# Other places in SBUF, modulo 256 bytes, for the operands of a block matmul stream

## The reference

```python
xn = _rmsnorm(h, norm_w)
proj = jnp.einsum('bsd,de->bse', xn, w_in).astype(f32)      # 2048 -> 14352 columns
q, k, v_m, o_m, z_m, i_pre, f_pre, u_g, v_g, z_g = _split_cols(proj)
...                                                          # mLSTM of 8 heads, gated unit of 8 heads
y = jnp.concatenate([y_m, y_g], axis=-1).astype(x.dtype)
h = h + jnp.einsum('bse,ed->bsd', y, w_out)                  # 4096 -> 2048
```

## Time and profile before

| | |
|---|---|
| median of 3 runs | 3193.33 us (3190.05 to 3199.09) |
| profiled execution | 3189.83 us, its span 3188.3 us |
| PE busy | 3127.2 us, 98% of the span |
| granted clock of TensorE | 0.996 of full speed over the span |
| block stages: SGU, mLSTM, output | 185 to 555, 555 to 1263, 1313 to 1428.5 us |

### The profile page before, as it was taken

One profiled execution on the slowest core, in us unless ns is written; L12 is line 12 of the kernel. 1 busy time (PEld: TensorE's weight loads), 2 busy tenths in 40 slices (PEclk: granted clock), 3 DMA queues, 4 the chain that ended last, 5 costly groups with the idle time before them and its releaser, 6 DMA issues.

```text
span 3188.3 us, 59876 instructions
## 1 busy us (share of the span) xinstructions
PE 3127.2 (98%) x23182; PEld 2929.1 (92%) x23182; DVE 2205.0 (69%) x2929; ACT 1548.3 (49%) x2506; POOL 334.4 (10%) x343
## 2 busy tenths in 40 slices
PE   8999999999999999999989999999999999999998
PEld 6899999999999998898889999999998888888898
DVE  7678888888888888876775656656457456556535
ACT  5355555555555556442263655556226455545421
POOL 1000000000000000000000341350000124313000
PEclk9999999999999999999999999999999999999999
DMA  6234444434434345453334222223324322222432
GB/s 208 89 96 106 113 112 112 126 92 112 113 98 118 93 118 178 121 160 106 106 117 135 62 73 81 81 75 106 113 94 151 103 79 80 80 74 68 165 97 90
DMA packets 461728, 342.81 MB, mean 108 GB/s; under 512 B 20504, under 2 KB 451544, under 8 KB 458352
## 3 DMA queue, kind: packets, MB, share of 16 engines
q1 hardware_dynamic: 443712, 296.28, 32.3%
q0 software_dynamic: 8304, 26.92, 2.4%
q10 hardware_dynamic: 9552, 17.37, 1.6%
HBM read 315.04 MB, written 25.46 MB: 107 GB/s over the span
## 4 chain that ended last, share of the span: by engine, by line
PE 82%; DVE 6%; DMA 4%; DVEq 3%; issue 2%; ACT 2%; SPq 0%; ACTq 0%
PE ps L756 13%; PE ps L757 13%; PE ps L758 13%; PE ps L926 8%; PE ps L929 8%; PE ps L928 8%; DMA w_raw_blocks<-in_w_in 3%; PE ps L1179 2%; PE ps L1340 1%; PE ps L1342 1%; PE ps L1338 1%; PE ps L762 1%; PE ps L996 1%; PE ps L764 1%; PE ps L763 1%
## 5 line engine op out<-in xcount | busy, mean ns | idle before, releaser
L756 PE MATMUL ps<-x_high,w_high 128*128 128x264 f32 (+3 forms) x2880 | 913.7, 317 | 19.7 <-DVE x_low L2590 10.7
L757 PE MATMUL ps<-x_low,w_high 128*128 128x264 f32 (+3 forms) x2880 | 882.6, 306 | 0.0
L758 PE MATMUL ps<-x_high,w_low 128*128 128x264 f32 (+3 forms) x2880 | 880.9, 306 | 0.0
L2101 DVE TENSOR_TENSOR w_low<-w_raw,w_high 128x1024 fp32r<-128x1024 f32 x308 | 377.8, 1233 | 330.2 <-ACT w_high L1380 315.0
L756 PEld LDWEIGHTS ps<-x_high,w_high 128*128 128x128 f32 x2880 | 544.1, 189 | 52.1 <-issue 22.4
L757 PEld LDWEIGHTS ps<-x_low,w_high 128*128 128x128 f32 x2880 | 544.3, 189 | 28.0 <-issue 3.3
L758 PEld LDWEIGHTS ps<-x_high,w_low 128*128 128x128 f32 x2880 | 542.5, 188 | 24.8
L926 PE MATMUL ps<-x_high_rows,w_high_blocks 128*128 128x256 f32 x1792 | 507.5, 283 | 4.2 <-DVE u_gelu L2224 2.9
L928 PE MATMUL ps<-x_low_rows,w_high_blocks 128*128 128x256 f32 x1792 | 498.8, 278 | 0.0
L929 PE MATMUL ps<-x_high_rows,w_low_blocks 128*128 128x256 f32 x1792 | 498.8, 278 | 0.0
L1380 ACT ACTIVATE w_high<-w_raw 128x1024 fp32r<-128x1024 f32 x308 | 324.7, 1056 | 277.3 <-PE ps L758 202.4
(11 more groups left out here) (523 smaller groups left out, 5328.5 us busy)
## 6 DMA issues: line engine op xcount, KB each, us to landing
w_raw_blocks<-in_w_in SPq DMA_DIRECT2D x200, 512.0 KB, 5.0
w_raw<-in_w_in SPq DMA_DIRECT2D x384, 256.0 KB, 3.1
w_raw<-in_w_out SPq DMA_DIRECT2D x224, 256.0 KB, 3.0
w_raw_blocks<-in_w_out SPq DMA_DIRECT2D x24, 512.0 KB, 5.6
residual<-residual_stream ACTq DMA_DIRECT2D x8, 1056.0 KB, 10.4
residual_stream<-y_layer ACTq DMA_DIRECT2D x2, 2176.0 KB, 11.6
x_natural<-in_x SPq DMA_DIRECT2D x4, 1024.0 KB, 9.4
x_feature_major<-x_stage POOLq DMA_DIRECT2D x4, 1024.0 KB, 7.9
```

Source lines behind the costliest of these rows:

```text
L756: pe.matmul(dst, wh[:, j, kt, wc], x_hi[:, k, tok], start=first, stop=False)
L757: pe.matmul(dst, wh[:, j, kt, wc], x_lo[:, k, tok], start=False, stop=False)
L758: return pe.matmul(dst, wl[:, j, kt, wc], x_hi[:, k, tok], start=False, stop=last)
L2101: dve.tensor_tensor(wl[:, j], raw[:, j], f(wh[:, j]), ALU.subtract).then_inc(lo_ready, 1)
```

## The change

No instruction is added, taken away or moved: each engine has the same instructions in the same order (line numbers of the new kernel are 7 to 11 higher). What changes are addresses. The weight slots are put 4,112 bytes apart in place of 4,096, so that slot 0 to 3 start at 128, 144, 160 and 176 modulo 256, in `whb` and `wlb` alike. The activations stay at 64. S2 goes to 128, S1 to 192, S3 to 0; S3 of the output stage stays at 64. `w_low` moves on by 256 bytes and `w_raw` by 512, both still at 128. Everything behind them moves by a few hundred bytes: the scratch tensors of the first layer from 64 mostly to 0 or 32, the residual stream and `y_layer` of the later layers from 64 to 128, with the small tensors of attention at 32, 64, 96, 128, 160, 192 or 224. `x_high`, `x_low`, `w_high` and `w_low`, the operands of the plain units, keep their places modulo 256, but for the last piece of weights (`w_high_last`, 64 to 128).

Moving minus stationary becomes, for slot j: 192-16j with the activations, 0-16j (modulo 256) with S2, 64-16j with S1, 128-16j with S3. These are the 16 multiples of 16, one for each of the pairs; in the mLSTM stage every kind of block meets every slot. From a block to the next the difference changes, while before it never did.

```diff
+        r0.at += 256
         wl_at = r0.at
         wl = r0.take("w_low", [P, 4, 4, 256], F32R)
+        r0.at += 256
         raw_at = r0.at
...
-        whb = nc.alloc_sbuf_tensor_at("w_high_blocks", [P, 4, KH, P], F32R, offset=wh_at)
-        wlb = nc.alloc_sbuf_tensor_at("w_low_blocks", [P, 4, KH, P], F32R, offset=wl_at)
+        def slots_at(name, at_):
+
+            room = nc.alloc_sbuf_tensor_at(name, [P, 4 * KH * P + 16], F32R, offset=at_)
+            slot = lambda j: slice(j * (KH * P + 4), j * (KH * P + 4) + KH * P)
+            return [room[:, slot(j)].rearrange("p (k n) -> p k n", k=KH) for j in range(4)]
+
+        whb, wlb = slots_at("w_high_blocks", wh_at), slots_at("w_low_blocks", wl_at)
...
-        ROWS_AT = 64
-        big = r0.at + (ROWS_AT - r0.at) % 256
-        x1_at = [at_ + (ROWS_AT - at_) % 256 for at_ in (xh_at, xl_at)]
+        def placed(at_, residue):
+            return at_ + (residue - at_) % 256
+
+        R_X, R_S2, R_S1, R_S3, R_S3_OUT = 64, 128, 192, 0, 64
+        big = placed(r0.at, R_S2)
+        x1_at = [placed(at_, R_X) for at_ in (xh_at, xl_at)]
...
-        ym_at = big + KT * S * 4
+        ym_at = big + KT * S * 4 + 64
...
-        work = ym_at + KT * S * 4
+        work = ym_at + KT * S * 4 + 96
...
-        for n, name in ((B_S2, "s2"), (B_S1, "s1"), (B_S3, "s3")):
+        for n, name, residue in ((B_S2, "s2", R_S2), (B_S1, "s1", R_S1), (B_S3, "s3", R_S3)):
+            rx_.at = placed(rx_.at, residue)
...
-        rs = Region(big + 6 * BLOCK)
+        rs = Region(rx_.at)
...
-        work2 = r2.at
+        work2 = r2.at + 160
...
-        S3G = big + 77824
+        S3G = placed(rn.at + BLOCK, R_S3_OUT)
...
-                    w_hi, w_lo = whb[:, slots[i]], wlb[:, slots[i]]
+                    w_hi, w_lo = whb[slots[i]], wlb[slots[i]]
...
-                act.activation(whb[:, slot], weight(s, i), ACT.Copy).then_inc(hi_ready, 1)
+                act.activation(whb[slot], weight(s, i), ACT.Copy).then_inc(hi_ready, 1)
...
-                dve.tensor_tensor(wlb[:, slot], weight(s, i), f(whb[:, slot]), ALU.subtract).then_inc(lo_ready, 1)
+                dve.tensor_tensor(wlb[slot], weight(s, i), f(whb[slot]), ALU.subtract).then_inc(lo_ready, 1)
```

## The result

The changed kernel takes 3205.80 us (median of 7 executions, 3203.97 to 3208.87), the kernel before 3195.48 us on the same chip (7 executions, 3190.05 to 3199.09): a ratio of 1.0034 with a 95% interval of 1.0025 to 1.0044. That is 10.3 us slower, a little past the 0.3% within which the prediction counted a time as the same. The profiled execution of the changed kernel took 3207.86 us.

What follows compares the result with a forecast made beforehand. PE's matmul pace was taken to bound the kernel (busy 3127.2 of 3188.3 us). The block stream's +2.6 us, other parts 0, on the 3193.33 us median gave 3196, written as 3195 us; range 3171 to 3216 us.

Steps and rivals of the forecast that it cites:

- the case that was called likeliest: Whole kernel: same time within 0.3%, at 3195 us, from even fresh landings or places that don't matter; chance 0.37 together.
- every other relation is heavy: Block matmuls: only difference 192 has the quick pace, others run at 117.8 ns; +21 us, 3203 to 3214 us, chance 0.26.
- the all-quick to the all-heavy end: Block stream: all blocks at 113.3 ns (quick) saves 21 us; all at 117.8 ns (heavy) loses 21 us.
- the sum: Whole kernel: all priced parts together, +2.6 us from the block stream and 0 from the others.
- the block stream: The 9,408 block matmuls: half the blocks land heavy as now, the other half start with three heavy matmuls; +2.6 us.
- The landing itself: At each of 392 block boundaries the changed difference makes the stream take a pace afresh, without a wait, neither preferred.
- places don't matter: Block stream: paces depend on when PE starts after a wait and last until the next; 3193 us, chance 0.12.
- Which stages: Block stages before the change: heavy share 0.19 in SGU, 0.74 in mLSTM and 0.13 in the output stage.
- What is late next: mLSTM: DVE's 2.7 us per block nearly level with all-quick PE's 2.72; a few of 18 us come back as waits.
- the rivals on the fast side: Block stream: shifts at boundaries end heavy runs but not quick ones; 3172 to 3183 us, chance 0.34.
- the writes to the slots: DVE's and ACT's writes at 16-byte steps: 0 us, low part stays 1,219 ns; slowed writes cost 10 us or more, chance 0.03.
- the other tensors: Attention's and the output's small tensors moved by multiples of 32: under 1 us, taken as 0.

Runs made afterwards that it cites:

- experiment 7: Changed kernel with all weight slots at 0, activations and sums at 64, so difference 64 in every block: 3202.72 us, ratio 1.0036 to the kernel before.
- experiment 1: Changed kernel with all slots at 144, activations and sums at 64, so difference 176 in every block: 3208.95 us against 3192.51 for the kernel before.
- experiment 2: Changed kernel with all slots back at 128, only the sums moved (differences 192, 0, 64, 128): 3202.45 us, ratio 1.0031 to the kernel before.
- experiment 5: Changed kernel with only the slots moved, all moving rows at 64 (differences 192, 176, 160, 144): 3204.27 us, ratio 1.0043 to the kernel before.
- experiment 6: Changed kernel with only slot 3 moved, 48 bytes on (difference 144, others 192), moving rows at 64: 3195.34 us, ratio 1.0010 to the kernel before.
- experiment 11: Changed kernel with slots at 140, 148, 152, 156, moving rows at 64 (differences 180, 172, 168, 164): 3200.71 us, ratio 1.0029 to the kernel before.
- experiment 9: Changed kernel with all slots at 140, activations and sums at 64, so difference 180 in every block: 3190.54 us against 3192.19 for the kernel before.
- experiment 3: Changed kernel with all slots at 160, activations and sums at 96, so difference 192 kept in every block: 3191.85 us, ratio 0.9995 to the kernel before.

## Why the prediction was right and where it was wrong

The time lies in the range, but the case that was called likeliest didn't come. The case called "every other relation is heavy", with a chance of 0.26, did. That the time is still only 10 us from the 3195 written is luck: the range reached nearly from the all-quick to the all-heavy end, and shorter stops, which the sum didn't have, took up part of a loss nine times as large as the sum's 2.6 us.

**The step that failed** is in the block stream: "Nothing in the rows prefers one pace at a landing, so half of the blocks land heavy, as now: 0 us." The address prefers. What was read as one stream with two paces is one difference, 192, with two; other differences have others, and of the 16 in the changed kernel only 192 and 64 showed a quick one at all. The mean distance over all block matmuls (those under 150 ns, so without stops) went from 115.6 to 118.2 ns. By stage that is 10.8 us in SGU, 9.2 in mLSTM and 4.1 in the output stage, 24 in place of the +2.6 of the sum; the rival's price for it was 21. The prediction named what would break its sum, paces other than 113.3 and 117.8 ns that last a whole block, and those are there, from 116.8 to 123.7 ns. The row that should have weighed more is the earlier trace rows: three groups whose differences aren't held at 192, all at the heavy end. Against them the prediction said that they never hold a difference for 24 matmuls. The third does: with rows at 64 as stationary operand and weights at 128 as the moving one, the difference is 64 in each of its matmuls. The timeline of before has them at the heavy pace:

```profile
119.80 0.28 PE L762 MATMUL ps<-w_high,x_high_rows 128*128 128x256 f32 x1
...
122.62 0.28 PE L762 MATMUL ps<-w_high,x_high_rows 128*128 128x256 f32 x1
```

24 matmuls lie between, 2.82 us / 24 = 117.5 ns, close to what experiment 7 found for 64 (117.8).

**The landing itself** is real. At a boundary without a wait the pace changes within a few matmuls, so "places don't matter" falls, with experiment 1 as the plainest proof. But a landing isn't a toss: it depends on what ran before (192: 23 of 23 quick from 144 in the mLSTM of the changed kernel, 33 of 34 heavy from 128 in experiment 2), and the difference before doesn't settle it alone (experiments 5, 6 and 11). The kernel before shows where its even split came from. At all 328 of its boundaries without a wait, where the difference doesn't change either, the pace stayed as it was; at 40 of the 63 behind a wait or other matmuls it changed. So in that kernel a pace lasts until the next wait at least, as the case "the places don't matter" had it.

**Which stages** could lose was read rightly from the earlier trace rows: SGU and the output stage were mostly quick and had most to lose per matmul, 3.6 and 4.1 ns against 1.7 in mLSTM.

**What is late next** was mis-sized. The prediction saw DVE and PE level in mLSTM at the quick pace and expected a few microseconds of a gain to come back. Experiment 9 shows that nearly all of it comes back, 20 us: DVE's low weights come late by up to 1.9 us at a time, and PE's clock falls behind three of the six longest waits. So the rivals on the fast side, 3172 to 3183 us, were out of reach for any choice of addresses tried here; the all-quick stream ends at 3190.5. The same cover works in the other direction: of the 24 us that the slower pace adds, the block stages grew by only 5.4 + 7.0 + 4.6 = 17 us, since the stops between blocks became shorter.

**The rest, between the 18 us of the profiled executions and the 10 us of the medians,** is mostly the profiled execution of before, which was a quick one of its kind. The kernels in which all blocks have one pace differ little from run to run (experiment 1 by 0.9 us, experiment 9 by 3.9), while the kernel before spreads over 9 us in 7 runs. That its share of quick blocks differs between executions would explain it, but there is one trace of it, so this is argued and not shown.

**Right at nothing:** the writes to the slots (1,219 ns as before), and the other tensors, whose moves left the time behind the output stage at 1760.2 us against 1760.0.

The Trainium skill, "TensorE: Matmul & The Clock Gate", Part 2, step 1, has the moving operand and the next weights read through two independent ports. By that rule alone experiment 1 would equal the kernel before; it runs at 118.7 ns with the same shapes, the same clock and another distance between the two operands. The trace disagrees, then: either the two reads do meet somewhere, or something else hangs on that distance, and no run here tells which.

The Trainium skill, "SBUF — State Buffer", Specifications, has lines of 16 bytes and a penalty for crossing into a new one. The slots of experiment 9 begin 12 bytes into such a line, and their blocks have the quick pace, with weight loads of 188 to 190 ns against 188 to 189 before; no penalty shows for contiguous operands.

**What stays open** is why a difference has the pace that it has. The distances within a block fall into short patterns (117, 117, 130 ns again and again at 208; 117, 123 at 16), which looks like reads of two streams that meet at fixed places, but no run here separates that from another cause. How far back the state of the stream reaches is open too, and so is the modulus: that 256 bytes is the period was assumed from the start and is hardly tested (only by the low weights of experiment 3).

## What to carry to other kernels

Where a matmul stream with a weight load for each matmul bounds a kernel, the distance modulo 256 bytes between its moving and stationary operands is a number to measure, not a detail of the allocator: here it decided between 113 and 124 ns. One distance held throughout is easier to reason about than several, because a block's pace also depends on the blocks before it. And before working on a stream's pace, look at what feeds it: with DVE's low weights as they are, a pace 2 ns quicker ended at the same time.

## What the hardware showed unexpectedly

- At one shape and a clock of 1.00, matmuls of 256 columns have at least seven paces that last a block: 113.3, 116.8, 117.8, 118.7, 120.0, 123.7 ns and about 118.3 at differences of 80, 188 and 240. The difference counts, not the places, for the one shift tried (32 bytes, experiment 3).
- Steps of 4 bytes matter as much as steps of 16: 118.3, 118.5 and 113.3 ns at 188, 184 and 180, then 118 at 164 and a quick pace again at 168.
- A pace is a state that outlasts a block. 180 ran at the quick pace in 388 of 392 blocks when held throughout, and at 120.0 ns in 56 of 70 when entered from 164 without a wait.
- Of six waits of 1.82 to 1.87 us in one execution, three were followed by some 3.4 us at 1.2 GHz, 1.6 us lost each beside the wait itself, and three by none.
